# Order of weight loads, first pair and first gate weights in the feed-forward part of a one-core decoder step

## The chip, the cores and the metric

The kernel runs on one core of a Trainium2 chip as one program. TensorE (PE) multiplies matrices, VectorE (DVE), ScalarE (ACT) and GpSimd (POOL) do elementwise work, SyncE (SP) issues most DMAs and ScalarE some. Each engine works off its own list of instructions in order and waits on semaphores. The metric is the device time of one execution in microseconds, median of several runs; less is better.

## The reference

One decoder layer for 1024 prompt tokens and 8 decode tokens, 1024 channels, all float32. The part that matters here is its second half:

```python
h = h + jnp.einsum('btnd,de->bte', g * pb, w_out)          # output projection

u = rmsnorm(h, g_mlp) @ w_up                               # matrix one, 1024 x 4096
h = h + jnp.square(jax.nn.relu(u)) @ w_down                # matrix two, 4096 x 1024

h = h + (p_l @ w_ple) * jax.nn.sigmoid(rmsnorm(h, g_ple) @ w_ple_gate)
return rmsnorm(h, g_final)
```

In front of it stand the input projections, stick-breaking attention, mLSTM and a short convolution, with paged caches for the decode tokens. The change doesn't touch them.

## The kernel before

**Arithmetic.** Every float32 product is made of three faster ones: each operand is rounded to a high part (`fp32r`) and the rest is its low part, and hi x hi, hi x lo and lo x hi are summed in PSUM. So all weights and activations are rounded (ScalarE or GpSimd) and subtracted (GpSimd or VectorE) before TensorE takes them.

**Matrix one and two** (`FeedForward`, from L1970) use a recursion with seven block products in place of eight (`PRODUCTS`, L1801: 1, 5, 6, 2, 7, 3, 4), over token halves, feature halves and channel halves. The 1032 tokens are two halves of 516, each taken in two pieces of 258. A *pair* is 256 output channels. Matrix one has 16 pairs (`UPS`), n = 0 to 15, each 7 products of 24 matmuls. Matrix two has 8 groups (`DOWN_GROUPS`) of 4 pairs (q = 0 to 3), each 7 products of 12 matmuls. For the seven products of a pair VectorE forms four sums of quarters of the raw weights (`form_sum`, L2039), ScalarE rounds seven weights (`round_weight`, L2067), GpSimd makes five low parts and VectorE two (`low_part`, L2056). Four weight slots are reused within a pair, so rounding waits for an earlier product.

**Activations.** The plain operands (products 1, 2, 3) and mixed ones (5, 6, 7, 4) of the normalised input lie in SBUF as `z_plain` and `z_mixed`. The mixed ones are differences of token halves (`form_operand`, L2142) that ScalarE rounds (`t_hi`, L2382) and VectorE subtracts (`t_lo`, L2653). After each pair of matrix one, VectorE adds what belongs together and applies the ReLU and the norm (`open_11`, `open_22`, `open_12`, `open_21`), ScalarE squares, VectorE forms differences (`mixed`), and seven operands are rounded and subtracted (`u_hi`, `u_lo`) into four slots `h[:, 4:8]`. From there SyncE stores them to the DRAM tensor `feed_forward_operands` (L2134, 516 KB each). `u_hi` waits until the slot's earlier store has landed. For matrix two ScalarE's queue issues the loads of a group's seven operands (`load_operand`, L2136, 1032 KB each); half b = 0 or 1 of `z_plain` and `z_mixed` is filled while the other is used. The first group's loads follow the products of the last pair of matrix one (`first_load`); the second group's are issued in pair q = 1 of the first group (`first_extra`).

**Raw weights.** Matrix one uses two buffers of 1 MB by turns (`raw_even`, and `w_raw` as `raw_odd`), matrix two half of each (512 KB a pair). SyncE's order in the loop (L2182 to L2188) is: load of pair n+2, stores 1 to 6 of pair n, store 0 of pair n+1, load of pair n+3, and so on. Each load waits for the low parts of the buffer's former pair.

**Around it.** `MixOut` (L1839) is the output projection: eight blocks of 128 channels, three chunks of tokens. VectorE adds each chunk to the residual, ScalarE rounds the block, VectorE subtracts, ScalarE squares and scales it, VectorE sums the squares, and SyncE stores the block to `residual`. After every second block VectorE forms the mixed differences. GpSimd splits the block weights. Behind it the first pair starts: `split_first` on GpSimd (L2080), two roundings and the `t_hi` on ScalarE (L2388 to L2419), a product order as in all pairs, the norm's three sums of squares by matmul after product 1 (L2291), and three roots on ScalarE (`root`). Before the stores of pair 0 go on, SyncE loads back `h[:, 0:4]` (L2181, 2 MB). In the last group `finish` rounds and squares each finished quarter and GpSimd adds the squares; `split_landed` (L108) then splits the first gate weights, block `e0`, on GpSimd, and `gates(0)` (L2942) begins.

## Time and profile before

| | us |
|---|---|
| median of 3 runs | 2052.49 (2048.16 to 2055.67) |
| the profiled execution | 2053.93 |
| its span | 2052.2 |
| TensorE busy | 1947.3 (95%) |
| VectorE busy | 1156.5 (56%) |
| GpSimd busy | 743.7 (36%) |
| ScalarE busy | 683.7 (33%) |

The output projection ends at 1152.5 us, matrix one runs from there to 1533.4 and matrix two to 1898.5. In the profile a row of a timeline is start, duration, engine, line, operation, output<-inputs, and in brackets how long the engine was idle before it and what ended that. PE is a matmul, SPq and ACTq a DMA issue. Matmuls overlap, so their durations are longer than their distance. All lines are those of the kernel before.

### The profile page before, as it was taken

To read this page: it belongs to the slowest core of one execution; us is meant where nothing else is said; L and a number is where in the kernel's file an instruction comes from. 1 tells how busy PE (TensorE), PEld (TensorE's weight loads), DVE (VectorE), ACT (ScalarE), POOL (GpSimd) and SP (SyncE) were. 2 spreads that over 40 slices of the span, in tenths; PEclk is the share of its full clock that TensorE was granted. 3 is DMA by queue.
4 is the path that set the end of the run, shared out by engine and by line. 5 is a ranking of instruction groups with operands and counts; after the bars stand their busy time and mean duration, and the time that the engine had idled before them with its cause. 6 is when DMAs were issued, how large, how long until landed. Compare 5 with 4: busy or idle time off the path is not lost.

```text
span 2052.2 us, 37980 instructions
## 1 busy us (share of the span) xinstructions
PE 1947.3 (95%) x13592; PEld 1899.3 (93%) x13592; DVE 1156.5 (56%) x1769; ACT 683.7 (33%) x1327; POOL 743.7 (36%) x580
## 2 busy tenths in 40 slices
PE   8999999999999999999999789999985999999897
PEld 7999999999999999999999789899885999999897
DVE  5101443456454666535565667767763666678357
ACT  5112333321112222222232444454543344446212
POOL 2323222222232222234472334444442344447523
PEclk9999999999999999999999999999997999999998
DMA  3441111135533565577563156566679557661313
GB/s 116 134 134 38 51 52 63 62 95 176 154 117 114 164 184 160 163 151 226 181 207 103 52 182 220 203 217 207 205 281 347 187 197 254 243 233 43 112 32 124
DMA packets 246847, 317.42 MB, mean 155 GB/s; under 512 B 19613, under 2 KB 179465, under 8 KB 238804
## 3 DMA queue, kind: packets, MB, share of 16 engines
q1 hardware_dynamic: 223028, 234.67, 36.8%
q10 hardware_dynamic: 23712, 81.31, 11.2%
q8 instruction: 69, 1.13, 0.2%
q14 instruction: 38, 0.31, 0.0%
HBM read 219.46 MB, written 96.50 MB: 154 GB/s over the span
## 4 chain that ended last, share of the span: by engine, by line
PE 22%; issue 13%; POOL 8%; DMA 3%; DVE 3%; ACT 1%; POOLq 0%; DVEq 0%; SPq 0%; ACTq 0%
POOL w_lo L2059 6%; PE acc L142 5%; PE turned_banks L2121 5%; PE acc L2959 4%; PE acc L2121 3%; PE n_sums L2121 3%; DMA w_raw<-in_w_down 1%; POOL h L2223 1%; PE n_sums L2979 1%; DMA feed_forward_operands<-h 1%; DMA raw_even<-in_w_down 1%; DVE h L2153 1%; PE turned_banks L2998 0%; DVE h L2692 0%; POOL sq_sum L2259 0%
## 5 line engine op out<-in xcount | busy, mean ns | idle before, releaser
L142 PE MATMUL acc<-x_hi,w_hi 128*128 128x344 f32 x1680 | 546.0, 325 | 1.8 <-DVEq L1796 1.2
L142 PE MATMUL acc<-x_hi,w_lo 128*128 128x344 f32 x1680 | 537.4, 320 | 0.0
L142 PE MATMUL acc<-x_lo,w_hi 128*128 128x344 f32 x1680 | 536.9, 320 | 0.0
L112 POOL TENSOR_SCALAR w_hi<-w_raw 128x1024 fp32r<-128x1024 f32 (+1 forms) x110 | 114.3, 1039 | 671.0 <-PE acc L142 465.6
L2121 PE MATMUL turned_banks<-z_mixed,w_hi 128*128 128x258 f32 x1536 | 293.3, 290 | 46.4 <-DVE w_lo L2059 14.6
L142 PEld LDWEIGHTS acc<-x_hi,w_hi 128*128 128x128 f32 x1680 | 316.6, 188 | 3.2 <-issue 2.3
L142 PEld LDWEIGHTS acc<-x_lo,w_hi 128*128 128x128 f32 x1680 | 316.4, 188 | 0.0
L142 PEld LDWEIGHTS acc<-x_hi,w_lo 128*128 128x128 f32 x1680 | 316.2, 188 | 0.0
L2121 PEld LDWEIGHTS turned_banks<-z_mixed,w_hi 128*128 128x128 f32 x1536 | 241.3, 193 | 56.9 <-ACT kept_products L2328 15.6
L115 POOL TENSOR_TENSOR w_lo<-w_raw,w_hi 128x1024 fp32r<-128x1024 f32 (+1 forms) x110 | 248.2, 2256 | 9.2
L2121 PE MATMUL turned_banks<-z_mixed,w_lo 128*128 128x258 f32 x768 | 219.5, 286 | 0.0
L2121 PE MATMUL acc<-z_plain,w_hi 128*128 128x258 f32 x1024 | 193.8, 288 | 12.1 <-POOL w_lo L2059 11.5
L2121 PEld LDWEIGHTS acc<-z_plain,w_hi 128*128 128x128 f32 x1024 | 161.6, 193 | 15.2 <-issue 10.8
L2059 POOL TENSOR_TENSOR w_lo<-weight_sums,w_hi 128x256 fp32r<-128x256 f32 (+1 forms) x96 | 96.6, 1006 | 155.4 <-ACT w_hi L2078 155.4
L2121 PEld LDWEIGHTS turned_banks<-z_mixed,w_lo 128*128 128x128 f32 x768 | 148.1, 193 | 0.0
L2121 PE MATMUL acc<-z_plain,w_lo 128*128 128x258 f32 x512 | 146.2, 286 | 0.0
L2059 POOL TENSOR_TENSOR w_lo<-raw_even,w_hi 128x256 fp32r<-128x256 f32 (+1 forms) x72 | 79.2, 1100 | 97.9 <-ACT w_hi L2078 97.9
L2059 POOL TENSOR_TENSOR w_lo<-w_raw,w_hi 128x256 fp32r<-128x256 f32 (+1 forms) x72 | 77.5, 1076 | 98.4 <-ACT w_hi L2078 98.4
L2356 ACT ACTIVATE h<-quadrants 128x516 fp32r<-128x516 f32 (+1 forms) x96 | 67.1, 699 | 100.1 <-DMA feed_forward_operands<-h 66.8
L2121 PE MATMUL n_sums<-z_mixed,w_hi 128*128 128x258 f32 x512 | 95.3, 284 | 3.9 <-issue 2.5
L2121 PEld LDWEIGHTS acc<-z_plain,w_lo 128*128 128x128 f32 x512 | 98.8, 193 | 0.0
L2121 PE MATMUL n_sums<-z_plain,w_hi 128*128 128x258 f32 x512 | 95.2, 285 | 0.0
(365 smaller groups left out, 3720.1 us busy)
## 6 DMA issues: line engine op xcount, KB each, us to landing
feed_forward_operands<-h SPq DMA_DIRECT2D x112, 516.0 KB, 3.9
z_mixed<-feed_forward_operands ACTq DMA_DIRECT2D x32, 1032.0 KB, 6.8
w_raw<-in_w_in SPq DMA_DIRECT2D x64, 512.0 KB, 4.3
z_plain<-feed_forward_operands ACTq DMA_DIRECT2D x24, 1032.0 KB, 5.4
page<-in_cache_k SPq DMA_DIRECT2D x64, 256.0 KB, 3.2
page<-in_cache_v SPq DMA_DIRECT2D x64, 256.0 KB, 2.7
merge_gate<-merge_gates SPq DMA_DIRECT2D x22, 516.0 KB, 3.7
merge_gates<-gate_out ACTq DMA_DIRECT2D x18, 516.0 KB, 3.8
```

The costliest lines, as they stand in the source:

```text
L112: nc.gpsimd.tensor_scalar(k.w_hi[:, par, 0:kb, :], k.w_raw[:, par, 0:kb, :], 1.0, 1.0, ALU.mult, ALU.mult).then_inc(k.w_rounded, 1)
L115: nc.gpsimd.tensor_tensor(k.w_lo[:, par, 0:kb, :], k.w_raw[:, par, 0:kb, :], k.w_hi[:, par, 0:kb, :].bitcast(F32), ALU.subtract).then_inc( ...
L142: mm = k.nc.tensor.matmul(k.acc[:, c, 0:CW], w[:, par, i, :], x[:, i, cols], start=(i == 0 and j == 0), stop=(i == kb - 1 and j == 2))
L2059: op(self.slot(pair, o, self.k.w_lo), self.weight_source(pair, o), self.slot(pair, o, self.k.w_hi).bitcast(F32), ALU.subtract).then_inc(se ...
L2121: mm = nc.tensor.matmul(self.bank(j)[:, e, 0:UNIT], w[:, i, :], x, start=(fresh and i == 0 and step == 0), stop=(i == len(tiles) - 1 and s ...
L2153: self.k.nc.vector.tensor_tensor(out, at(a), at(b), ALU.subtract).then_inc(self.s["t_ready"], 1)
L2223: op(h[:, 4 + r, HALF:TT].bitcast(F32R), quads[:, quad, :], h[:, 4 + r, 0:HALF], ALU.subtract)\
L2356: nc.scalar.activation(h[:, 4 + first:4 + first + count, 0:HALF].bitcast(F32R), self.quads[:, quad:quad + count, :], ACT.Copy)\
L2959: mm = nc.tensor.matmul(k.acc[:, bank_of(u), 0:n], w[:, par, i, :], x[:, i, cols], start=(i == 0 and step == 0), stop=(i == KD - 1 and ste ...
L2979: mm = nc.tensor.matmul(emb_bank(u)[:, 0:n], w[:, i, m * P:(m + 1) * P], x[:, i, cols], start=(i == 0 and step == 0), stop=(i == KP - 1 an ...
```

## The change

Names change with it: a helper `after(n, j)` gives the number of products done when product j of pair n is, because the first pair now has an order of its own; parameters named `after` become `following`. The moves are these.

- SyncE in matrix one: the load of pair n+3 is issued after store 5 of pair n, ahead of store 6 of pair n and store 0 of pair n+1. The load of pair 2 goes ahead of the 2 MB `residual` load.
- Matrix two's raw weights: pair q has a buffer of its own (halves of `raw_even` for q = 0, 1, of `w_raw` for q = 2, 3), with its own semaphore, and each load waits for the pair four before it. The first two are loaded before the stores of pair 14 end, the next two before the stores 1 to 6 of pair 15.
- In the last pair of matrix one, ScalarE's roundings `u_hi(last, 0)` and `u_hi(last, 1)` go behind the operand loads. VectorE and GpSimd leave more of that pair's remainder to the first pairs of matrix two. The second group's seven loads spread over pairs 1 to 3.
- First pair: product order 1, 5, 2, 6, 7, 3, 4. GpSimd forms all four sums first, squares the last block and adds its squares. Two weights are rounded, and the operand of product 5 is rounded and subtracted, before the last block's own rounding. The norm's sums follow product 2.
- In the output projection the differences of blocks 2k-2, 2k-1 are formed at the start of block 2k+1, and `scale_block` stands ahead of the next block's rounding.
- The first gate weights go to `raw_even`, ScalarE rounds and VectorE subtracts them in pair q = 2 of the last group.

```diff
+                if b % 2 and b > 1:
+                    for j in (5, 7, 6, 4):
+                        ffn.form_operand(dve, j, b // 2 - 1)
...
+                    if b == KD - 1 and c == 0:
+                        ffn.form_operand(dve, 5, KD // 2 - 1)
                 dve.drain().then_inc(s["h_done"], 1)
+                if b == KD - 1:
+                    ffn.before_last_split(dve)
...
+    def square_last(self, pool, op):
+        pool.wait_ge(self.s["h_done"], KD)
+        pool.wait_ge(self.s["sq_added"], KD - 1)
+        op(self.squares, self.h[:, KD - 1, :], self.h[:, KD - 1, :], ALU.mult).then_inc(self.s["squared"], 1)
+    def add_last(self, pool, op):
+        pool.wait_ge(self.s["squared"], KD)
+        op(self.k.sq_sum[:, :], self.k.sq_sum[:, :], self.squares, ALU.add).then_inc(self.s["sq_added"], 1)
...
+            if b:
+                self.scale_block(act, b - 1)
+            if b == KD - 1:
+                ffn.before_last_rounding(act)
...
+FIRST_PRODUCTS = (1, 5, 2, 6, 7, 3, 4)
+FIRST_WEIGHTS = (0, 1, 3, 2, 4, 5, 6)
...
+def after(n, j):
+    order = FIRST_PRODUCTS if is_first(n) else PRODUCTS
+    return n * NPROD + order.index(j) + 1
...
-        if pair.par:
-            return self.k.w_raw[:, 1, :, :].rearrange("p k n -> p (k n)").rearrange("p (k n) -> p k n", n=2 * P)
...
-        return self.raw_even[:, 0:4, :]
+        if pair.q < 2:
+            return self.raw_even[:, 4 * pair.q:4 * pair.q + 4, :]
+        return self.k.w_raw[:, pair.q - 2, :, :].rearrange("p k n -> p (k n)").rearrange("p (k n) -> p k n", n=2 * P)
...
-            act.wait_ge(s["product"], pair.n * NPROD + (o - 2 if o < 3 else -1 if o == 3 else o - 3))
+            act.wait_ge(s["product"], after(pair.n - (o < 4), PRODUCTS[{0: 4, 1: 5, 2: 6, 3: 3, 4: 0, 5: 1, 6: 2}[o]]))
...
+    def before_last_rounding(self, act):
+        first = self.up(0, 0, 0)
+        self.round_weight(act, first, 0)
+        self.round_weight(act, first, 1)
+        act.wait_ge(self.k.acc_ready, self.base * NCH + 2 * NCH)
+        self.t_hi(act, 5, 0)
+        self.t_hi(act, 5, 1)
+    def before_last_split(self, dve):
+        self.t_lo(dve, 5, 0)
+        self.t_lo(dve, 5, 1)
...
-        stores(0, 0, 0, (0,))
+        load(self.up(2, 0, 1))
         sp.wait_ge(s["t_lo"], 8)
         sp.dma_start(self.h[:, 0:4, :], self.k.h_back[:, 0:4, :]).then_inc(self.h_in[0], 16)
-        with sp.Fori(0, UPS // 2 - 1) as i:
-            load(self.up(i * 2 + 2, 0, i + 1))
-            stores(i * 2, i, 0, range(1, NPROD))
-            stores(i * 2 + 1, i, 1, (0,))
-            load(self.up(i * 2 + 3, 1, i + 1))
-            stores(i * 2 + 1, i, 1, range(1, NPROD))
-            stores(i * 2 + 2, i + 1, 0, (0,))
+        stores(0, 0, 0, (0,))
+        def pair_stores(n, g, kt, loads):
+            stores(n, g, kt, range(1, 6))
+            for pair in loads:
+                load(pair)
+            stores(n, g, kt, (6,))
+            stores(n + 1, g + kt, 1 - kt, (0,))
+        with sp.Fori(0, UPS // 2 - 2) as i:
+            pair_stores(i * 2, i, 0, [self.up(i * 2 + 3, 1, i + 1)])
+            pair_stores(i * 2 + 1, i, 1, [self.up(i * 2 + 4, 0, i + 2)])
         last = UPS - 1
-        load(self.down(0, 0, 0))
-        stores(last - 1, last // 2, 0, range(1, NPROD))
-        stores(last, last // 2, 1, (0,))
-        load(self.down(0, 0, 1))
-        stores(last, last // 2, 1, range(1, NPROD - 1))
-        load(self.down(0, 0, 2))
+        half = UPS // 2 - 1
+        pair_stores(last - 3, half - 1, 0, [self.up(last, 1, half)])
+        pair_stores(last - 2, half - 1, 1, [])
+        sp.wait_ge(s["w_lo"], last * 5)
+        for q in range(2):
+            self.load_raw(sp, self.down(0, 0, q))
+        pair_stores(last - 1, half, 0, [])
+        sp.wait_ge(s["w_lo"], UPS * 5)
+        for q in range(2, OUTS):
+            self.load_raw(sp, self.down(0, 0, q))
+        stores(last, half, 1, range(1, NPROD - 1))
...
-        load(self.down(0, 0, 3))
+        def down_load(g, b, q):
+            pair = self.down(g, b, q)
+            sp.wait_ge(s["w_lo"], pair.n * 5 - 15)
+            self.load_raw(sp, pair)
...
+        for i in range(1, 5):
+            self.form_sum(pool, op, first, i)
+        low(first, 0)
+        low(first, 1)
+        self.mix.square_last(pool, op)
+        low(first, 3)
+        self.mix.add_last(pool, op)
+        for o in (2, 4, 5, 6):
+            low(first, o)
...
+        u_lo(last, 0)
+        low(down0, 5)
+        low(down0, 6)
...
+            if j == 2:
                 pe.wait_ge(self.mix.s["sq_added"], KD)
-                for (cols, _), bank in zip(self.PIECES, self.norm_sums):
-                    nc.tensor.matmul(bank, k.ones[:, :], k.sq_sum[:, cols], start=True, stop=True).then_inc(s["n1_summed"], 1)
...
+        t_hi(act, 7, 0)
         root(0)
-        keep_5(0)
+        t_hi(act, 7, 1)
         self.round_weight(act, p0, 4)
         root(1)
+        t_hi(act, 4, 0)
         root(2)
+        self.round_weight(act, p0, 5)
         keep_u2(0)
-        t_hi(7, 0)
-        t_hi(7, 1)
-        self.round_weight(act, p0, 5)
+        t_hi(act, 4, 1)
         self.round_weight(act, p0, 6)
-        t_hi(4, 0)
-        t_hi(4, 1)
...
         first_load(5)
-        u_hi(last, 1)
         square(last, 2, 1)
         self.round_weight(act, down0, 2)
         first_load(6)
-        def down_pair(pair, after, extra, first=False):
+        u_hi(last, 0)
...
+        second_load = {(1, 4): 0, (1, 6): 1, (2, 1): 2, (2, 3): 3, (2, 5): 4, (3, 1): 5, (3, 3): 6}
...
+                if (q, o) == (2, 3):
+                    act.wait_ge(k.w_landed[0], self.gate_block // 2 * 16 + 16)
+                    act.wait_ge(s["product"], (UPS + g * OUTS) * NPROD)
+                    nc.scalar.activation(k.w_hi[:, 0, :, :], self.gate_raw(), ACT.Copy).then_inc(k.w_rounded, 1)
...
+        operand(dve, 7, KD // 2 - 1)
+        operand(dve, 6, KD // 2 - 1)
+        t_lo(dve, 6, 0)
+        t_lo(dve, 6, 1)
+        operand(dve, 4, KD // 2 - 1)
+        t_lo(dve, 7, 0)
+        t_lo(dve, 7, 1)
+        t_lo(dve, 4, 0)
         form_sum(p1, 1)
-        t_lo(4, 0)
+        t_lo(dve, 4, 1)
         form_sum(p1, 2)
-        t_lo(4, 1)
...
+        left = {(0, 1): (lambda: u_lo(last, 1),), (0, 2): (lambda: mixed(last, 0), lambda: mixed(last, 1)),
+                (0, 3): (lambda: u_lo(last, 2),), (0, 4): (lambda: u_lo(last, 3),),
+                (0, 6): (lambda: u_lo(last, 4), lambda: mixed(last, 2))}
...
+                if (q, o) == (2, 6):
+                    dve.wait_ge(k.w_rounded, self.gate_block + 1)
+                    nc.vector.tensor_tensor(k.w_lo[:, 0, :, :], self.gate_raw(), k.w_hi[:, 0, :, :].bitcast(F32), ALU.subtract)\
+                      .then_inc(k.w_split, 1)
...
-            gate_weights(0)
+            sp.wait_ge(done["w_lo"], (ALL - OUTS + 1) * 5)
+            sp.dma_start(ffn.gate_raw(), w_gate[:, :, 0:P]).then_inc(k.w_landed[0], 16)
...
-            split_landed(k, pool, e0, 0, e0 // 2)
```

## Rows read from the trace of the kernel before

**Rows 1.** Table of windows: stretch, length, busy us by engine, granted PE clock, DMA.
```profile
1152.50:1190.00 37.50, 27.12 (x179) 25.21 (x178) 29.64 (x28) 23.51 (x34) 17.65 (x11) 0.86 0.04 15
1190.00:1217.90 27.90, 22.09 (x170) 21.68 (x169) 17.14 (x21) 11.81 (x21) 9.51 (x8) 0.94 0.69 240
1217.90:1239.60 21.70, 20.88 (x170) 20.28 (x168) 16.27 (x21) 11.64 (x22) 9.52 (x8) 1.00 0.64 212
1239.60:1488.40 248.80, 233.20 (x1849) 224.49 (x1849) 176.00 (x210) 123.16 (x221) 113.28 (x78) 1.00 0.62 210
1488.40:1511.90 23.50, 21.25 (x168) 20.43 (x168) 15.90 (x20) 11.07 (x21) 10.19 (x8) 1.00 0.60 200
1511.90:1533.40 21.50, 20.70 (x169) 20.35 (x169) 14.66 (x18) 8.50 (x15) 9.31 (x7) 1.00 0.91 335
1533.40:1608.50 75.10, 47.67 (x337) 46.37 (x338) 33.13 (x56) 22.54 (x50) 18.52 (x22) 0.80 0.73 276
1608.50:1648.80 40.30, 39.50 (x330) 39.30 (x329) 26.89 (x47) 16.84 (x40) 16.29 (x20) 1.00 0.65 232
```
**Rows 2.** Waits, 1239.6 to 1488.4: total us, times, longest us.
```profile
ACT h L2356 <- DMA feed_forward_operands<-h: 36.4, 11, 4.0
DVE acc L2054 <- DMA raw_even<-in_w_up: 33.3, 6, 5.8
DVE acc L2054 <- DMA w_raw<-in_w_up: 28.0, 5, 6.1
```
**Rows 3.** DMA issues, 1239.6 to 1488.4: size and median us to landing.
```profile
feed_forward_operands<-h SPq DMA_DIRECT2D x77, 516.0 KB, 3.8
raw_even<-in_w_up SPq DMA_DIRECT2D x6, 1024.0 KB, 7.0
w_raw<-in_w_up SPq DMA_DIRECT2D x5, 1024.0 KB, 7.4
```
**Rows 4.** Timeline of one steady pair of matrix one, which starts at 1397.45.
```profile
1400.02 0.39 SPq L2065 DMA_DIRECT2D w_raw<-in_w_up  x1
...
1407.60 0.70 DVE L2054 TENSOR_TENSOR acc<-w_raw 128x512 f32<-128x512 f32 x1 [5.47 <-DMA w_raw<-in_w_up]
...
1408.97 0.64 ACT L2356 ACTIVATE h<-quadrants 128x516 fp32r<-128x516 f32 x1 [3.34 <-DMA feed_forward_operands<-h]
...
1416.84 0.69 DVE L2587 TENSOR_TENSOR quadrants<-n_sums,kept_products 128x516 f32<-128x516 f32 x1
...
1420.02 0.50 PE L2121 MATMUL acc<-z_plain,w_hi 128*128 128x258 f32 x2 [0.65 <-POOL w_lo L2059]
...
1426.27 0.52 PE L2121 MATMUL turned_banks<-z_mixed,w_hi 128*128 128x258 f32 x2 [0.23 <-ACT turned_banks L2319]
```
**Rows 5.** Timeline around the last two projection blocks and the first pair.
```profile
1130.66 2.41 POOL L115 TENSOR_TENSOR w_lo<-w_raw,w_hi 128x1024 fp32r<-128x1024 f32 x1
1131.07 3.10 DVE L1915 SCALAR_TENSOR_TENSOR z_plain<-h,g_mlp_c,z_plain 128x1032 fp32r<-128x1032 f32 x1 [1.28 <-ACT z_plain L1939]
...
1154.52 1.29 DVE L1915 SCALAR_TENSOR_TENSOR z_plain<-h,g_mlp_c,z_plain 128x1032 fp32r<-128x1032 f32 x1 [1.27 <-ACT z_plain L1939]
...
1157.43 1.05 ACT L2386 ACTIVATE z_mixed<-h 128x1032 fp32r<-128x1032 f32 x1
...
1158.80 0.77 PE L2280 MATMUL turned_banks<-z_plain,w_hi 128*128 128x258 f32 x2 [6.11 <-POOL w_lo L2059]
```
**Rows 6.** DMA view, 1510 to 1610, in 40 slices, and one timeline row.
```profile
GB/s 149 74 247 295 422 429 405 391 373 409 419 410 423 391 414 251 9 245 384 295 316 390 262 412 426 423 423 419 414 407 402 259 28 0 0 0 0 0 145 71
DMA packets 9559, 28.08 MB, mean 281 GB/s; under 512 B 592, under 2 KB 3664, under 8 KB 7504
...
1591.09 0.43 DVE L2054 TENSOR_TENSOR acc<-w_raw 128x256 f32<-128x256 f32 x1 [15.72 <-DMA w_raw<-in_w_down]
```
**Rows 7.** Timeline between matrix two and the first gate.
```profile
1902.16 0.75 DVE L2778 SCALAR_TENSOR_TENSOR z_lo<-h,g_ple_c,z_mixed 128x516 fp32r<-128x516 f32 x1 [0.80 <-ACT z_mixed L2538]
...
1905.13 2.34 POOL L115 TENSOR_TENSOR w_lo<-w_raw,w_hi 128x1024 fp32r<-128x1024 f32 x1
...
1907.53 0.69 PE L2959 MATMUL acc<-z_mixed,w_hi 128*128 128x384 f32 x1 [8.99 <-POOL w_lo L115]
```

More of the change, by code:

```diff
@@ L2043, in form_sum @@
         if i == 1:
-            eng.wait_ge(self.raw_in[pair.par], pair.half * 16 + 16)
+            eng.wait_ge(*self.landed(pair))
         if i in (2, 4):
@@ L2224, in u_lo, with steady @@
                 .then_inc(s["u_lo_pool"], 1)
-        def steady(pair, after):
+        def steady(pair, following):
             for o in (2, 3, 5, 6):
@@ L2229, in steady @@
             u_lo(pair.n - 1, 6)
-            low(after, 0)
+            low(following, 0)
             u_lo(pair.n, 0)
-        self.split_first(pool, self.up(0, 0, 0))
+        first = self.up(0, 0, 0)
+        for i in range(1, 5):
[7 more added lines that the diff above has]
+            low(first, o)
         low(self.up(1, 1, 0), 0)
@@ L2239, in gpsimd @@
         last = UPS - 1
-        steady(self.up(last, 1, UPS // 2 - 1), self.down(0, 0, 0))
         for o in (2, 3, 5, 6):
-            low(self.down(0, 0, 0), o)
+            low(self.up(last, 1, UPS // 2 - 1), o)
+        u_lo(last - 1, 6)
+        down0 = self.down(0, 0, 0)
+        for o in (0, 2, 3):
+            low(down0, o)
+        u_lo(last, 0)
+        low(down0, 5)
+        low(down0, 6)
         u_lo(last, 6)
@@ L2357, in u_hi, with steady @@
               .then_inc(s["u_hi"], 1)
-        def steady(pair, after):
+        def steady(pair, following):
             n = pair.n
@@ L2581, in open_whole, with open_sum @@
               .then_inc(s["read"], 1)
-        def open_sum(n, o, j, kept, other, quad, i):
-            dve.wait_ge(s["product"], n * NPROD + o)
+        def open_sum(n, j, kept, other, quad, i):
+            dve.wait_ge(s["product"], after(n, j))
             dve.wait_ge(s["kept"], n * 3 + kept)
@@ L2631, in u_lo, with steady @@
                                     h[:, 4 + first:4 + first + count, 0:HALF], ALU.subtract).then_inc(s["u_lo"], 1)
-        def steady(pair, after):
+        def steady(pair, following, spare=None):
             n = pair.n
@@ L2706, in next_sum @@
             def next_sum(i):
-                if after is not None:
-                    form_sum(after, i)
+                if following is not None:
+                    form_sum(following, i)
             previous()
@@ L2728, in down_pair @@
             add_read(n, 6, 3, 2 * q, 1)
-            if after is not None:
-                low_part(after, 1)
+            if following is not None:
+                low_part(following, 1)
             extra(6)
@@ L2755, in group @@
                     previous = before_q
[L2756 removed]
+                down_pair(pair, following, previous, extra(q))
         for q in range(OUTS):
```

210 lines of the change are left out of this document (104 added, 106 removed).

## The prediction, made before the changed kernel was run

> **What bounds the kernel now.** I read the page's slices first: TensorE is busy nearly throughout, so only its holes and stretches of lower granted clock can be won. The table of windows, cut at the borders of the stages, then says where the holes are. The group stage of matrix two, undisturbed, runs four pairs (336 matmuls) in 40.3 us [rows 1]: 0.12 us a matmul, so 20.2 us for a pair of matrix one (168 matmuls) and 10.1 us for a pair of matrix two (84). Against this, eleven steady pairs of matrix one take 248.8 us, 22.6 each [rows 1], though no engine but TensorE is full (VectorE 176.0 us, GpSimd 113.3). The first pair takes 37.5 us counted from the last projection matmul, the second 27.9, the last one and the first four of matrix two 96.6 (21.5 + 75.1) instead of 20.2 + 40.3 = 60.5 [rows 1].
>
> The list of waits for the steady stretch shows what is late: VectorE waits 33.3 + 28.0 us for raw weights, 5.6 us in each of eleven pairs, and ScalarE 36.4 us for stores [rows 2]. A load lands after 7.0 to 7.4 us, a store after 3.8 [rows 3]. In the timeline the load of the pair after next is issued at 1400.02, lands at 1407.60 and holds VectorE 5.47 us. The store issued just behind it holds ScalarE until 1408.97. From then VectorE works without a hole, opens the last sum at 1416.84, and weights for the next pair come late on GpSimd; TensorE starts the next pair at 1420.02 [rows 4].
>
> **Part 1, steady pairs.** Before, the load of pair m stands in SyncE's queue behind the store of operand 0 of pair m-2. Now it stands behind operand 5 of pair m-3 and waits only for the low parts of pair m-2. Nothing is added or dropped: each pair has its 1 MB load and seven stores. I laid out the queues of one pair at 20.2 us, from its first matmul as zero. The last raw weights of a pair are split at about 11.5 us, so the load is issued there and has until 4 us into the next pair, 12.7 us; it needs 7.4 [rows 3]. VectorE's 5.6 us wait goes. The two stores that now stand behind the load (operands 6 and 0) become ready at 15 and 18 us, later than the load's issue, and are needed at 3.4 and 5.9 us of the next pair: 8 us each against 3.8 [rows 3]. The store of operand 1 no longer shares the engines with a load.
>
> What is late next? The longest chain is the one around the pair's end: open the last sum, finish the quadrants, differences, round, then seed the bank of product 6. It runs from 1416.84 to 1426.27, 9.43 us [rows 4], of which about 0.8 us is waiting for ScalarE and GpSimd, which are early once VectorE is. That leaves 8.6 us, and three products give TensorE 8.65. So it just fits; VectorE has 16.0 us of work in 20.2. I take 20.4 us a pair, between 20.2 (no hole) and 21.5 (the chain stays at 9.4 and another hole of 0.5 remains). The pair before the eleven and the eleven are 21.7 + 248.8 = 270.5 us [rows 1], and 12 x 20.4 = 244.8: **25.7 us**, bounds 12 and 28. The last pair but one, 23.5 [rows 1] to 20.3: **3.2 us**.
>
> **Part 2, first pair.** The stall of 6.11 us before the first matmul is for a weight that ScalarE rounds only after block 7 [rows 5]. Now two weights, the first two rounded halves of the operand of product 5 and both their low parts lie inside the last projection block, where ScalarE waits for chunks. What is left is the last chunk's add, 0.9 us. The low parts of the operand of product 5 are VectorE's and start when GpSimd squares the last block. A GpSimd instruction over 1024 columns took 2.41 us, and a VectorE one of the same width started 0.4 us later took 3.10 us instead of 1.29 [rows 5]: it ended 1.1 us after GpSimd. So the low part waits for the square, and product 5 starts 2 us after product 1 ends. The Trainium skill states this as a rule (SBUF — State Buffer, "Who interferes with whom"): two engines share a port pair, held for a whole instruction, against an instruction with two SBUF inputs. The trace agrees, 3.10 against 1.29; by the free duration the pair would be 2 us shorter.
>
> Then the order 1, 5, 2 lets the plain product run while the mixed operands are made, the norm sums come after it (about 1.3 us), and product 7 waits for the second kept product, which stands in ScalarE's queue behind three roots and four operand roundings: about 3 us. Sum from the last projection matmul: 0.9 + 20.2 + 2 + 1.3 + 3 + 2 (slower clock after the holes, half of what 0.86 granted cost before) = 29.4 instead of 37.5: **8 us**, bounds 4 and 11.
>
> The second pair had 27.9 us because the load of the third was issued behind the 2 MB residual. That load now goes first: 21 us, **7 us**, bounds 4 and 7.7.
>
> **Part 3, matrix one to matrix two.** Four raw pairs instead of two can be in flight, the first operand loads are taken ahead of two roundings in ScalarE's queue, and the second group's seven loads (7.2 MB) move from pair 1 to pairs 1 to 3. Worst before was the wait of 15.72 us for the fourth raw weights, issued into a queue full of those loads [rows 6]; that goes. What stays is the amount: 28.08 MB move between 1510 and 1610, and the transfers run at about 410 GB/s when they are dense [rows 6]. That is 68.5 us, more than TensorE's 60.5. VectorE also has the leftovers of the last pair in the first pair of matrix two (about 12 us of work in 10), so a hole of 2 to 3 us there lies beside the same time. I take the transfers as the bound: 68.5 instead of 96.6, **28 us**. Bounds: 36 at no stall, 18 if the transfers have as many thin slices as before, when they ended at about 1590 [rows 6] and group 1 could not have started sooner. The last of the second group's loads is issued some 5.5 us before group 1 starts and all seven are awaited at once, so the hole will be there.
>
> The Trainium skill (DMA: Bandwidth & Descriptors, "Queues, rings and completion order") says that SyncE's and ScalarE's queues have a ring each on the same 16 engines, which alternate between them. Then a deeper queue of raw weights brings no bytes faster, only earlier. The throughput row is flat at 373 to 429 GB/s in its dense stretches, whichever queue feeds it [rows 6]; by queues independent of each other this part would be worth 36 us.
>
> **Part 4, gate weights.** TensorE waits 8.99 us at the first gate for a GpSimd instruction that ends at 1907.47 and stands behind all its adds of squares [rows 7]. The rounding (ScalarE, 1.05 us by the row of the same size) and the subtraction (VectorE, at most 1.29 us) [rows 5], now lie in the last group's third pair. VectorE is 67 per cent busy in the undisturbed group, 26.9 us in 40.3 [rows 1], more in the last; they may cost up to 1 us there. Next late is the low part of the last quadrant, 1902.91 [rows 7], which the first gate awaits before its last block: 0.6 us. The second weights follow 3 us earlier on GpSimd, the embedding's stay where they were and are due just then. **8 us**, bounds 3 and 9.
>
> Sum: 25.7 + 3.2 + 8 + 7 + 28 + 8 = 79.9 us. The profiled execution took 2053.9 us (span 2052.2), 1.4 over the median of 2052.5; so 1974 profiled, and I forecast **1974 us**, leaving the 1.4 us to parts that I rounded up.
>
> **The rivals.** (a) The transfers are not dense at the border: stores wait for VectorE's leftovers and the second group waits for its last load. Part 3 gives 18: 1984 us. For it: between its dense stretches the throughput fell to 9 and 245 GB/s [rows 6]; against: raw weights and first loads no longer queue behind stores. (b) The steady chain does not shrink: ScalarE and VectorE run 9.4 us from the last sum to the seed and TensorE waits 0.8 us there and again for GpSimd's weight. Pairs of 21.5, 12 and 1 of them: 1988 us. Both together: 1998. (c) Slower: the load blocks SyncE. It waits for all low parts of the pair before, and the stores behind it hold ScalarE's rounding ahead of the kept product, which TensorE needs. It decides from the point where these stores land over 8 us late; to lose, each of 14 pairs must grow by 5.7 us over my 20.4, for example to 27: 2066. Against: the load's condition is met at 11.5 us, those stores are ready at 15. (d) The load doesn't move: the low parts it waits for end together with the store that it stood behind, so part 1 goes: 2003. Against: GpSimd is through with them and does three more instructions before that store is ready.
>
> **Numbers.** Forecast 0.50, (a) 0.18, (b) 0.15, both 0.06, (d) 0.05, (c) 0.02, better than forecast 0.04 (all bounds good: 1958). The range 1958 to 2001 leaves out less than 2 in 10. One measurement of this kernel tells about 0.3% (6 us) from no change: faster 0.96, same 0.02, slower 0.02.
>
> **What would show it.** Steady pairs of 20.2 to 20.6 us and no wait of VectorE for raw weights; the first matmul of matrix one within 1 us of the last projection matmul; a hole before product 7 of the first pair; one hole, of a few us, before group 1 of matrix two, with transfers near 410 GB/s until then; the first gate within 1 us of the last product. Wrong would be: pairs above 21.5, ScalarE still waiting for stores, or several holes of over 3 us behind 1533.

## The result, and the profile after

The changed kernel takes 1980.1 us (median of 4 runs, 1976.5 to 1981.1), the kernel before 2053.4 us in the same comparison: a ratio of 0.9643, 95% interval 0.9621 to 0.9666. Forecast was 1974 us in a range of 1958 to 2001. The profiled execution has a span of 1979.3 us, 72.9 less than before.

The table of windows of the changed kernel, cut at the same borders as [rows 1] (stretch, length, busy us of TensorE, its weight loads, VectorE, ScalarE and GpSimd with their counts, granted clock, DMA share, GB/s):

```profile
1152.90:1183.80 30.90, 25.06 (x180) 23.36 (x180) 25.89 (x24) 21.27 (x32) 16.87 (x9) 0.94 0.25 92
1183.80:1203.90 20.10, 20.10 (x169) 20.10 (x169) 16.81 (x20) 11.82 (x20) 10.62 (x7) 1.00 0.81 287
...
1225.90:1466.10 240.20, 240.20 (x2004) 240.20 (x2003) 203.59 (x227) 141.08 (x239) 130.62 (x84) 1.00 0.66 231
1466.10:1486.30 20.20, 20.20 (x171) 20.20 (x170) 14.17 (x19) 10.29 (x19) 8.87 (x6) 1.00 1.02 376
1486.30:1511.20 24.90, 13.95 (x84) 13.38 (x82) 14.04 (x21) 9.26 (x19) 6.45 (x8) 0.79 0.89 346
1511.20:1546.30 35.10, 32.29 (x254) 32.09 (x255) 21.69 (x36) 12.65 (x30) 14.24 (x17) 0.95 0.93 346
1546.30:1586.60 40.30, 40.30 (x326) 40.30 (x326) 26.22 (x45) 15.78 (x38) 15.70 (x18) 0.96 0.66 231
```

What to see: from 1183.8 to 1486.3 TensorE is busy as long as the stretch is, in every row. The steady pairs have no hole left. The stretch that took 75.1 us before [rows 1] is the fifth and sixth row here, 24.9 + 35.1 = 60.0 us, with TensorE busy in only 46.2 of them and a granted clock of 0.79 in the first. This is what is left of the stalls, most of it in and just behind the first pair of matrix two.

By the starts of TensorE's products, the gain is made up of: projection to second pair 37.6 to 30.9 us (6.7); second pair 27.9 to 20.2 (7.8); the 14 pairs behind it 315.5 to 282.4 (33.1, of which 1.3 in the last pair); the first four pairs of matrix two 75.1 to 60.0 (15.1); the rest of matrix two 0.6; the tail from the start of the last product of matrix two to the end 155.3 to 145.6 (9.7). The projection ended 0.25 us later, which leaves 72.8; the spans rounded give 72.9.

The list of waits of the steady stretch of the changed kernel, 1225.9 to 1466.1 (total us, times, longest us), its three longest:

```profile
POOL w_lo L2113 <- ACT w_hi L2132: 73.9, 48, 2.4
ACT quadrants L2442 <- DVE quadrants L2674: 40.4, 18, 3.3
POOL h L2306 <- ACT h L2456: 36.4, 12, 3.0
```

The three rows of [rows 2], waits for raw weights and for stores, are not in it, though loads and stores take as long as before; the view of the DMA issues of the same stretch:

```profile
feed_forward_operands<-h SPq DMA_DIRECT2D x83, 516.0 KB, 3.8
w_raw<-in_w_up SPq DMA_DIRECT2D x6, 1024.0 KB, 6.8
raw_even<-in_w_up SPq DMA_DIRECT2D x5, 1024.0 KB, 6.9
```

Against [rows 3] the times from issue to landing are nearly the same (3.8, 6.8 and 6.9 us against 3.8, 7.4 and 7.0); what changed is when the loads are issued.

In the first pair of matrix two the timeline of the changed kernel shows where TensorE stands:

```profile
1488.97 0.63 ACT L2456 ACTIVATE h<-quadrants 128x516 fp32r<-128x516 f32 x1 [2.26 <-DMA feed_forward_operands<-h]
...
1491.06 0.49 PE L2162 MATMUL turned_banks<-z_mixed,w_hi 128*128 128x258 f32 x2 [1.99 <-ACT turned_banks L2419]
...
1494.89 0.63 ACT L2456 ACTIVATE h<-quadrants 128x516 fp32r<-128x516 f32 x1 [3.67 <-DMA feed_forward_operands<-h]
...
1500.75 0.77 PE L2162 MATMUL turned_banks<-z_mixed,w_hi 128*128 128x258 f32 x2 [5.05 <-ACT kept_products L2428]
...
1509.16 1.32 POOL L2306 TENSOR_TENSOR h<-quadrants,h 128x516 fp32r<-128x516 f32 x1 [7.23 <-ACT h L2456]
...
1511.21 0.51 PE L2162 MATMUL acc<-z_plain,w_hi 128*128 128x258 f32 x2 [3.93 <-POOL w_lo L2113]
```

ScalarE's roundings at 1488.97 and 1494.89 write the slots that pair 14's stores are read from, and wait for those stores: the one issued at 1477.44 took 17.4 us and landed at 1494.81, just ahead of the second rounding. The seed and the copies that TensorE needs stand behind these roundings in ScalarE's queue, so the first two stalls go back to stores. The third, ahead of the second pair, does not do so directly: GpSimd's low part of the weights stands behind the last pair's operand (the row at 1509.16), which waited 7.23 us for ScalarE's rounding, and that rounding for VectorE's difference. This is the leftover work of the last pair.

A *hole* is, in what follows, the distance from the start of the last matmul before it to the first one behind it, less the 0.12 us that two matmuls are apart at full speed. It is some 0.15 us longer than the idle time in brackets, which counts from a modelled end (0.47 longer behind the norm's matmuls).

The view of the transfers from 1466.3 to 1546.3 (40 slices of 2 us) shows the rest:

```profile
GB/s 244 236 370 430 426 404 414 419 405 416 423 418 414 425 417 381 379 349 58 383 386 281 74 256 316 155 281 413 400 390 407 408 420 401 406 409 407 425 378 133
DMA packets 10204, 28.31 MB, mean 354 GB/s; under 512 B 607, under 2 KB 4693, under 8 KB 8150
```

Behind the first three slices the transfers are dense, at about 412 GB/s, until 1502, thin until 1520, and dense again until the group's operands have landed. At 412 the 28.31 MB are 68.7 us; they took 80.

### The profile page after: what moved, and what is told of

Read it like the earlier page. It is cut to its first block and busy times, and to the rows that moved or that the text cites. A ratio compares the mean times of both kernels' runs of the same rounds, so it can differ in the third digit from the quotient of the medians.

```text
span 1979.3 us, 37940 instructions
## 1 busy us (share of the span) xinstructions
PE 1926.6 (97%) x13592; PEld 1890.7 (96%) x13592; DVE 1181.8 (60%) x1769; ACT 693.0 (35%) x1327; POOL 760.1 (38%) x580
## 3 DMA queue, kind: packets, MB, share of 16 engines
q1 hardware_dynamic: 223028, 234.67, 37.6%
q10 hardware_dynamic: 23712, 81.31, 11.7%
## 5 line engine op out<-in xcount | busy, mean ns | idle before, releaser
L2162 PE MATMUL turned_banks<-z_mixed,w_hi 128*128 128x258 f32 x1536 | 286.4, 285 | 15.2 <-ACT kept_products L2428 8.0
L2113 POOL TENSOR_TENSOR w_lo<-weight_sums,w_hi 128x256 fp32r<-128x256 f32 (+1 forms) x96 | 111.8, 1164 | 186.0 <-ACT w_hi L2132 186.0
L2113 POOL TENSOR_TENSOR w_lo<-w_raw,w_hi 128x256 fp32r<-128x256 f32 (+1 forms) x72 | 81.7, 1135 | 48.1 <-ACT w_hi L2132 48.1
L142 PE MATMUL acc<-y_hi,w_hi 128*128 128x344 f32 x288 | 93.3, 324 | 1.9 <-POOL w_lo L115 1.1
```

The costliest lines, as they stand in the source:

```text
L142: mm = k.nc.tensor.matmul(k.acc[:, c, 0:CW], w[:, par, i, :], x[:, i, cols], start=(i == 0 and j == 0), stop=(i == kb - 1 and j == 2))
L2113: op(self.slot(pair, o, self.k.w_lo), self.weight_source(pair, o), self.slot(pair, o, self.k.w_hi).bitcast(F32), ALU.subtract).then_inc(se ...
L2162: mm = nc.tensor.matmul(self.bank(j)[:, e, 0:UNIT], w[:, i, :], x, start=(fresh and i == 0 and step == 0), stop=(i == len(tiles) - 1 and s ...
```

## The experiments

All ran against the kernel before; ratios are to it, the changed kernel having 0.9643. "Four pairs" is the time from the first product of matrix two to the first one of its group 1, from the profile. The intervals are 3 to 5 us wide to each side, so where kernels differ by less the profile decides.

**Undo the order of SyncE's queue (e5).**

```diff
-            stores(n, g, kt, range(1, 6))
-            for pair in loads:
-                load(pair)
-            stores(n, g, kt, (6,))
+            stores(n, g, kt, range(1, 7))
             stores(n + 1, g + kt, 1 - kt, (0,))
+            for pair in loads:
+                load(pair)
```

> Only SyncE's order in matrix one's loop is put back: the load of the raw weights stands behind the last store of its pair and the first store of the next, instead of ahead of them. Nothing is left out. If the order of SyncE's queue is what the steady pairs gained by, the pairs go back from 20.17 us to 22.0 to 22.6, on 11 to 13 pairs, and the time is 2004 to 2012. If the pairs gained by something else (product order, the shorter chain around the first pair, fewer waits), they stay at 20.2 to 20.6 and the time is 1979 to 1985.

2011.1 us, ratio 0.9798 (0.9775 to 0.9820): 31.8 us of the gain gone. Twelve pairs that took 242.0 us take 268.2, 22.35 each. The waits of 1230 to 1470 in this kernel are those of [rows 2] again, within a microsecond:

```profile
ACT h L2455 <- DMA feed_forward_operands<-h: 37.1, 11, 3.7
DVE acc L2108 <- DMA raw_even<-in_w_up: 33.3, 6, 5.9
DVE acc L2108 <- DMA w_raw<-in_w_up: 27.7, 5, 5.8
```

So the place of the load, ahead of two stores or behind them, is the cause of the steady gain. Matrix one, first pair included, lost 36.5 us, but the four pairs at the border took 55.3 instead of 60.0 us. I take it that slower pairs ahead leave less in flight at the border; no run tests that.

**Undo the hand-over of the gate weights (e6).**

```diff
# ScalarE's and VectorE's parts in the last group taken out; GpSimd, behind its last add of squares (waits left out here):
+        nc.gpsimd.tensor_scalar(k.w_hi[:, 0, :, :], self.gate_raw(), 1.0, 1.0, ALU.mult, ALU.mult).then_inc(k.w_rounded, 1)
+        op(k.w_lo[:, 0, :, :], self.gate_raw(), k.w_hi[:, 0, :, :].bitcast(F32), ALU.subtract).then_inc(k.w_split, 1)
```

> The first gate weights (128x1024) are rounded and split by GpSimd behind its last part of matrix two, as in the kernel before, instead of by ScalarE and VectorE inside the last group; the load keeps its new place and buffer. Nothing is left out. If the 9.7 us that the tail gained come from this hand-over, they go back: the first gate product starts 8 to 11 us later than 1.5 us after the last product of matrix two; time 1987 to 1992. If they come from the earlier load alone: 0 to 3 us; time 1979 to 1983.

1989.2 us, ratio 0.9687 (0.9666 to 0.9708): 9.0 us. The timeline of this kernel has a row like that of [rows 7] again:

```profile
1841.74 2.34 POOL L2373 TENSOR_TENSOR w_lo<-raw_even,w_hi 128x1024 fp32r<-128x1024 f32 x1
...
1844.14 0.69 PE L3053 MATMUL acc<-z_mixed,w_hi 128*128 128x384 f32 x1 [9.30 <-POOL w_lo L2373]
```

The early load alone gives nothing; the engine that splits does.

**ScalarE's copies first (e1).** The roundings of the last pair's operands move behind the copies in all three engines' queues.

```diff
-        left = {(0, 0): square(last, 3, 2), (0, 1): u_hi(last, 1), (0, 2): u_hi(last, 2), (0, 3): u_hi(last, 3), ...
+        left = {(0, 0): square(last, 3, 2), (0, 3): u_hi(last, 0), (0, 5): u_hi(last, 1), (1, 0): u_hi(last, 2), ...
```

> ScalarE's roundings of the last pair's operands (u_hi of the pair before matrix two) stand behind the seed and the two copies of the first pair of matrix two, instead of ahead of them; VectorE's and GpSimd's parts of the same chain move with them. Nothing is left out. Theory 1 (order): the holes of the first pair (2.15, 5.20 and 4.09 us) come from ScalarE, which waits in order for stores to land while TensorE waits for the copies behind. Then the first pair takes 10 to 13 us instead of 24.9, what waits next is the residual, and the four pairs of group 0 take 52 to 56 us instead of 60.0; time 1972 to 1976. Theory 2 (bytes): the transfers are the bound whatever the order; the holes move to the second and third pair, where VectorE waits for the residual, and the four pairs stay within 58.5 to 61.5; time 1978 to 1982.

1978.4 us, 0.9631 (0.9615 to 0.9647), four pairs 59.4 us. Both totals lie in the ranges of theory 2. Of the mechanism each theory got half: the first pair falls from 25.2 to 14.8 us as theory 1 said, and the third rises from 10.1 to 19.7, as theory 2 said. In this kernel's timeline VectorE then stands for the residual, and TensorE behind it:

```profile
1513.31 0.34 SPq L2275 DMA_DIRECT2D h<-residual  x1
...
1522.70 0.70 DVE L2788 TENSOR_TENSOR h<-turned_banks,h 128x516 f32<-128x516 f32 x1 [9.95 <-DMA h<-residual]
...
1524.22 0.77 PE L2162 MATMUL turned_banks<-z_mixed,w_hi 128*128 128x258 f32 x2 [7.72 <-ACT turned_banks L2420]
```

**The second group's loads early (e2), and both (e3).**

```diff
-        second_load = {(1, 4): 0, (1, 6): 1, (2, 1): 2, (2, 3): 3, (2, 5): 4, (3, 1): 5, (3, 3): 6}
+        second_load = {(1, o): o for o in range(NPROD)}
```

> The seven loads of the second group's operands are issued in the second pair of matrix two, one at each product, as in the kernel before, instead of being spread from the second pair to the fourth. Nothing is left out. Theory 3 (spread): the transfers are thin from 1501 to 1520 us and the hole of 2.96 us ahead of group 1 is the price of the spreading; then the hole goes, the thin stretch fills, and the four pairs take 55 to 57.5 us instead of 60.0; time 1975 to 1977. Theory 2 (bytes) and theory 1: the seven loads (1 MB each) run beside the last stores and the residual, which land later, and VectorE waits for the residual at the third pair: 61 to 66 us; time 1981 to 1986.

> The edits of the two runs before together: ScalarE's copies first, and the second group's loads in the second pair. Nothing is left out. Theory 1: 48 to 54 us for the four pairs, since the second pair now starts some 12 us earlier and the second group's loads with it; time 1968 to 1974. Theory 2 (bytes): what the one gains the other takes: 58 to 62 us; time 1978 to 1983.

e2: 1978.1 us, 0.9637 (0.9621 to 0.9653), four pairs 58.9 us. The hole ahead of group 1 is gone, a smaller one came in the fourth pair. It gained 1 us of the 2.5 to 5 that theory 3 asked, and had none of the loss that the other two forecast; all three missed. e3: 1986.4 us, 0.9676 (0.9660 to 0.9693), four pairs 67.7 us, worse than any theory said. With ScalarE early the seven loads meet the last stores. The view of the DMA issues of e3, 1494 to 1544 (count, KB each, median us to landing), and then the timeline of its longest wait:

```profile
z_mixed<-feed_forward_operands ACTq DMA_DIRECT2D x4, 1032.0 KB, 9.1
feed_forward_operands<-h SPq DMA_DIRECT2D x6, 516.0 KB, 11.0
```

```profile
1530.69 0.69 DVE L2788 TENSOR_TENSOR h<-turned_banks,h 128x516 f32<-128x516 f32 x1 [17.73 <-DMA h<-residual]
...
1532.21 0.77 PE L2162 MATMUL turned_banks<-z_mixed,w_hi 128*128 128x258 f32 x2 [13.48 <-ACT turned_banks L2420]
```

A store of 0.5 MB takes 11.0 us there against 3.8 in the steady pairs; the residual load has to wait for it in SyncE's queue, and VectorE for the residual.

**Fewer bytes (e4).**

```diff
-        act.dma_start(self.ops.rows(j, b, 0, 0, 4).bitcast(F32), src).then_inc(sem, 16)
+        act.dma_start(self.ops.rows(j, b, 0, 0, 4)[:, 0:rows, :].bitcast(F32), src[:, 0:rows, :]).then_inc(sem, 16)   # rows=1 for group 0
```

> Each of the seven loads of the first group's operands carries one of its four rows (0.26 instead of 1.06 MB); the other three rows of group 0's operands are left as they were, so this part of matrix two is not computed from its data. 5.5 MB less at about 400 GB/s is 14 us of transfer. Theories 1 and 2 (contention): pair 14's stores land in 4 us, as in the steady pairs, instead of 8, ScalarE doesn't wait, and the four pairs take 43 to 48 us instead of 60.0; time 1962 to 1968. Theory 4 (the stores are late by themselves, by the order in which SyncE issues them, six in 17 us): ScalarE waits as before, the holes of the first pair stay above 8 us, and the four pairs take 55 us or more.

1973.9 us, 0.9617 (0.9600 to 0.9633), four pairs 55.0 us. That is outside the range of theories 1 and 2 and at the edge of theory 4's, but of ScalarE's waits for stores in the first pair (2.26 and 3.67 us) only one of 1.27 us is left, against theory 4. 5.4 MB less gave 5 us, not 14. Stores issued from 1461 to 1495 landed in 4.8 us (median) instead of 10.0 in the changed kernel (1466 to 1500), so it is shown that the stores are late because of the loads beside them. But TensorE still had holes of 3.08 us ahead of product 7 and 3.83 ahead of the second pair, now behind the last pair's differences and roundings themselves. In this kernel's timeline:

```profile
1489.05 1.06 ACT L2456 ACTIVATE h<-quadrants 128x1032 fp32r<-128x1032 f32 x1 [2.87 <-DVE quadrants L2720]
...
1490.74 0.77 PE L2162 MATMUL turned_banks<-z_mixed,w_hi 128*128 128x258 f32 x2 [2.93 <-ACT kept_products L2428]
```

**The wait for the residual later (e7), and that with fewer bytes (e8).**

```diff
-            if q != 1:
-                dve.wait_ge(self.h_in[q == 2], 48 if q == 3 else 32)
             down_pair(...)
# and inside down_pair, after next_sum(2):
+            before_add()      # the same wait, ahead of add_kept
```

> The edit of e1 (ScalarE's copies first) with one more: VectorE's wait for the residual stands directly ahead of the first addition that needs it, instead of ahead of the whole pair (there it also held the last addition of the pair before, whose end ScalarE's seed waits for, and the sums of weights). Nothing is left out. Theory 2, as a chain: in e1 the second residual load was issued at 1513.3 us and landed at 1522.7, and TensorE stood 7.9 us. With the wait later TensorE goes two to three products further; 3 to 5 of the 7.9 us go, the four pairs take 54 to 57 us instead of 59.4, time 1973 to 1976. If the residual isn't what bounds (rather the sum of bytes up to group 1), the time comes back ahead of group 1: 58 to 60 us, time 1977 to 1980.

> The kernel of e7 with the small loads of e4 (each of the seven loads of group 0's operands carries one of its four rows; that group's product isn't computed from its data). If order and bytes together explain the 20 us that the four pairs take above their 40.3 at full speed, both are gone here: 41 to 46 us for the four pairs; time 1959 to 1965. If a third thing holds them (GpSimd's low parts, the clock), 50 us or more as in e4 (55.0).

e7: 1979.0 us, 0.9637 (0.9617 to 0.9658), four pairs 61.7 us. The third pair fell to 13.8 us, from e1's 19.7, the fourth rose to 21.6, from 12.3: the time came back ahead of group 1, as the second case said, and a little more than it said. e8: 1976.4 us, 0.9622 (0.9600 to 0.9644), four pairs 61.0 us: 15 us above the first range, so the second case in number (50 or more), and slower there than e4, from which it differs only in the two edits of order. In e8 the first pair took 10.4 us, full speed; then the second group's loads, issued from 1506.35 by a ScalarE that was now early, ran beside the last store (issued 1509.62; the residual load that waits for it went out at 1525.88), and the next raw weights stood in SyncE's queue behind both:

```profile
1525.88 0.34 SPq L2275 DMA_DIRECT2D h<-residual  x1
...
1526.67 1.22 SPq L2119 DMA_DIRECT2D raw_even<-in_w_down  x2
...
1537.13 0.43 DVE L2108 TENSOR_TENSOR acc<-raw_even 128x256 f32<-128x256 f32 x1 [11.65 <-DMA raw_even<-in_w_down]
```

**The second group's loads behind the residual (e9), and raw weights ahead of it (e12).**

```diff
# e9, over e7
+        second_load = {(2, 3): 0, (2, 4): 1, (2, 5): 2, (2, 6): 3, (3, 0): 4, (3, 1): 5, (3, 2): 6}
# e12, over e7
+        second_load = {(1, 1): 0, (1, 3): 1, (2, 3): 2, (2, 4): 3, (2, 5): 4, (2, 6): 5, (3, 0): 6}
+        down_load(1, 1, 0)
         residual(0, self.h_in[1])
         stores(last, last // 2, 1, (NPROD - 1,))
+        down_load(1, 1, 1)
         residual(2, self.h_in[0])
```

> The kernel of e7 with the second group's seven operand loads issued later: the first at the fourth product of the third pair of matrix two, the last early in the fourth, one at each step. Nothing is left out. Theory 5 (SyncE's chain): in e7 and e8 the last stores and the residual took 9 to 16 us to land beside these loads (1 MB each), and behind the wait for them stood the second residual load (issued 1528.7) and the next raw weights (landed 1540.2). With the loads behind the residual, the stores land in 4 to 5 us again, the third pair doesn't stand, and what is left is the landing of the second group: seven loads of 2.6 us from about 1518, so 1537 to 1541 on e7's clock: the four pairs take 50 to 55 us instead of 60.0, time 1970 to 1975. Theory 2 (the sum of bytes up to group 1 is the bound, whatever the order): 58 to 62 us, time 1978 to 1982.

> The kernel of e7 with two things more: SyncE issues the raw weights of group 1's first two pairs ahead of the residual loads instead of behind them (in e9 they were issued at 1516.1 beside seven operand loads and landed at 1536.5, and TensorE stood 12.3 us for them), and of the second group's seven operand loads two are issued at the start of the second pair, where the transfers were thin (240 GB/s from 1504 to 1513 in e9), and five from the middle of the third. Nothing is left out. In all four orders run so far the 80 us that end with group 1's first product carried 28.1 to 28.3 MB at 354 to 358 GB/s, where the dense slices show about 412: if thin stretches are what is left to win, this order takes up to 5 us of them: the four pairs take 53 to 57 us instead of 60.0, time 1973 to 1977. If each load that fills the thin stretch makes the last stores later by as much, as in e2 and e3, the four pairs take 59 to 62 us, and the time is 1978 to 1982.

e9: 1979.5 us, 0.9647 (0.9629 to 0.9664), four pairs 59.6 us. The stores did land early (the last issued 1508.73; the residual load behind it went out at 1515.33) and the first three pairs took 13.7, 12.0 and 10.1 us, but the raw weights behind the residual took 20.4 us to land beside the seven loads, and the fourth pair took 23.8. Theory 5 missed; both totals lie in theory 2's ranges. e12: 1981.9 us, 0.9655 (0.9641 to 0.9669), four pairs 63.2 us: the time is in its second case, the four pairs 1 us above it. The two loads at 1500.59 and 1503.38 hold the stores up, as in e3, and the second residual load is late:

```profile
1509.00 0.64 ACT L2458 ACTIVATE h<-quadrants 128x516 fp32r<-128x516 f32 x1 [4.80 <-DMA feed_forward_operands<-h]
...
1540.02 0.70 DVE L2783 TENSOR_TENSOR h<-h,kept_products 128x516 f32<-128x516 f32 x1 [8.65 <-DMA h<-residual]
```

**GpSimd beside VectorE in the first pair (e10).**

```diff
-        op(self.squares, self.h[:, KD - 1, :], self.h[:, KD - 1, :], ALU.mult).then_inc(self.s["squared"], 1)
+        pool.sem_inc(self.s["squared"], 1)
# and the addition of the square likewise
```

> GpSimd's square of the last block of the output projection and its addition to the sum of squares are left out (that block is missing from the normalisation); all the rest of the changed kernel stands. If VectorE's operations are long because GpSimd works beside them: the two t_lo of 1.84 us each fall to 1.2 to 1.4, product 5 of the first pair starts without its 0.94 us, the two differences of 2.29 us each fall to 0.7 to 1.5, and product 6 starts 1 to 1.9 us earlier; the first pair takes 28.5 to 30 us instead of 30.9. If they wait for something else (ScalarE's rounding, the scaling of the block), the durations stay and the two holes too.

One run, 1973.7 us. The timeline of the changed kernel, VectorE's rows and the GpSimd rows beside them:

```profile
1153.62 1.91 POOL L1937 TENSOR_TENSOR quadrants<-h 128x1032 f32<-128x1032 f32 x1 [3.35 <-DVEq L1918]
...
1154.08 3.68 DVE L2205 TENSOR_TENSOR z_mixed<-h,z_mixed 128x1032 fp32r<-128x1032 f32 x2 [0.58 <-ACT z_mixed L2199]
...
1160.09 2.41 POOL L1941 TENSOR_TENSOR sq_sum<-sq_sum,quadrants 128x1032 f32<-128x1032 f32 x1
...
1160.19 4.58 DVE L2194 TENSOR_TENSOR h<-h 128x516 f32<-128x516 f32 x2 [1.23 <-ACT h L1949]
```

and VectorE's two rows in e10's timeline:

```profile
1151.12 2.38 DVE L2205 TENSOR_TENSOR z_mixed<-h,z_mixed 128x1032 fp32r<-128x1032 f32 x2 [0.58 <-ACT z_mixed L2199]
...
1156.85 2.40 DVE L2194 TENSOR_TENSOR h<-h 128x516 f32<-128x516 f32 x2 [2.14 <-ACT h L1949]
```

3.68 becomes 2.38 us and 4.58 becomes 2.40, of the same two instructions each. The hole ahead of product 5 (0.94 us) is gone, that ahead of product 6 falls from 1.88 to 0.37, and the first pair, from the warm-up matmul, takes 27.3 instead of 29.85 us, both at a granted clock of 0.94 (from the last projection matmul, as the expectation counts, 28.3 instead of 30.9: a little below its range). So GpSimd's square and addition cost 2.5 us here, in two places. VectorE holds up GpSimd too: GpSimd's low part at 1158.27 took 1.85 us with VectorE's row of 1157.68 beside it (until 1158.96), and 1.31 in e10, where it ran alone. These rows agree with the Trainium skill's rule of the port pair (SBUF — State Buffer, "Who interferes with whom").

**The copy of U2 earlier (e11).**

```diff
-        root(2)
-        self.round_weight(act, p0, 5)
         keep_u2(0)
+        self.round_weight(act, p0, 5)
+        root(2)
```

> In the first pair, ScalarE's copy of U2 (keep_u2) stands ahead of the rounding of weight 5 and the last third of the root, instead of behind both. Nothing is left out. The hole of 3.2 us ahead of product 7 was waited for at this copy (idle 2.95 us, released by ScalarE). If ScalarE's order is the cause, product 7 starts 1.5 to 2.3 us earlier, and the first pair takes 28.8 to 30 us instead of 30.9, unless the root, now 1.2 us later, holds the fourth product of the bank behind it. If the operand or the low part of product 7 is as late as the copy, it stays at 30.5 or more. The time differs by less than its interval either way; the profile decides.

1979.1 us, 0.9645 (0.9628 to 0.9662). TensorE's idle time ahead of product 7 fell from 2.95 to 1.18 us and the first pair, from the warm-up matmul, from 29.85 to 27.2 us (28.2 as the expectation counts, below its range). Of the 2.6 us, 1.5 are the clock, as the last section shows. And the root, now later, gave holes of 0.56 us ahead of product 4 and 1.09 in the second pair, which rose from 20.2 to 21.4. First and second pair together take 48.6 us, as they do in e1, e2 and e3 with the old order and the same clock. No gain.

## Why the prediction was right, and where it was not

**Steady pairs**: predicted 25.7 + 3.2 us by 20.4 us a pair, measured 20.17 with no hole, 31.8 for the same pairs. The mechanism is the predicted one, shown by e5. The chain around the pair's end does fit into three products; the 0.2 us of caution, 13 times, are the difference; the twelve pairs alone gave 28.5, just above the upper bound of 28. Rivals (b), (c) and (d) did not occur.

**First pair**: predicted 8, measured 6.7; 30.9 us instead of 29.4. Its steps: product 5 came 0.94 us late, not 2, since GpSimd's square began 0.5 us ahead of VectorE and was over at 1155.5, so that it held only the first of two instructions; TensorE stood 2.95 us ahead of product 7 for the copy, as predicted (3). The step that was missing is product 6, with a hole of 1.88 us: I had counted the contention once, but the addition of the square and a low part lie beside the two differences as well (e10; what the low part alone costs was not tested). That the new order of products and weights gave the 6.7 us is read from the trace; no run puts it back.

**Second pair**: predicted 7, measured 7.8, full speed. Before, VectorE stood 9.68 us for the load issued at 1192.17, behind the 2 MB residual; now the load is issued at 1176.54, ahead of it, lands at 1181.9, and the wait is gone. No run undoes this move alone. **Gate weights**: predicted 8 with 9 as upper bound, measured 9.7; the first gate product follows the last product of matrix two without a wait, and TensorE is idle for 0.77 and 0.35 us later; e6 gives 9.0 for it.

**Border of the matrices**: the term that was mis-sized. "I take the transfers as the bound: 68.5 instead of 96.6" gave 28 us; measured were 20.2 + 60.0 = 80.2, so 16.4, which is below its own lower bound of 18. By the prediction's own signs this part was wrong: ScalarE still waited for stores there (2.26 and 3.67 us), and two holes were above 3 us. It is rival (a) with its reason: the amount was right (28.31 MB in the 80 us up to group 1), the density was not, 354 GB/s on average against 412 in the dense slices. I had put all of the hole ahead of group 1, which is 2.96 us; the others, 2.15, 5.20 and 4.09, lie in and behind the first pair of matrix two. What did come true is that VectorE's wait of 15.72 us for the fourth raw weights [rows 6], behind which TensorE had a hole of 11.7 us, is gone; which of the moves at the border did that was not tested. e2 puts one of them back, the spreading of the second group's loads, and loses nothing.

That the total came out 6 us from the forecast is in part luck: the border fell short by 11.6 us and the first pair by 1.3, and the steady pairs, the second pair, the gate weights and the rest of matrix two gave 6.0 more than forecast.

What the runs put in place of "the transfers are the bound": neither the amount nor one engine's order is. Taking 5.4 MB away gave 5 us (e4), and with two edits of order beside it nothing (e8, 61.0 us); an order of the same bytes took 67.7 (e3). Taking ScalarE's wait away gave 10 us in the first pair and lost 10 in the third (e1). What the traces show in each of these kernels is a chain through SyncE's queue: last pair's stores, which wait for the slots of the pair before; residual loads, which wait for those stores; raw weights behind both. Its links landed in 3 to 8 us with few loads beside them, and in 8 to 25 beside the 1 MB operand loads, which have a queue of their own. That this chain is the bound is my reading and not shown: no kernel removed it, and four forecasts built on it (e7, e8, e9, e12) missed, since each edit moved the wait to another link. Loads placed in the thin stretch make the links late (e3, e8, e12); loads placed behind it come late themselves (e9). Six orders of all the work gave 58.9, 59.4, 59.6, 61.7, 63.2 and 67.7 us against 60.0. The rule of the Trainium skill that the prediction weighed (DMA: Bandwidth & Descriptors, "Queues, rings and completion order") fits these rows: it says that the queues share the engines, and in e3 a store among the large loads takes 11.0 us instead of 3.8.

None of the complete kernels beat the changed one by more than its interval. Left open is whether smaller pieces (the residual in four loads, the group's products waiting for one operand each) would shorten the chain; that was not tried. Also open is how much of the thin stretch belongs to the leftover work of ScalarE, VectorE and GpSimd alone; that it holds TensorE is seen in the hole ahead of the second pair, 4.09 us and still 3.83 with the stores on time (e4).

## What to carry to other kernels

A load that waits behind a store in the same queue costs what the store waits for, not what it transfers; moving it ahead of two stores was worth 32 us here, the largest part of the 73. Where a stage is bound by bytes, look for the stretch in which the transfers are thin and ask which chain of dependent transfers crosses it: the bytes divided by the dense rate are a floor, and such a chain can keep you above it: here 80 us instead of 69. And price an engine's slow neighbour for every pair of instructions that lie side by side, not for the first.

## What the runs showed of the hardware that was not expected

The granted clock makes the same instructions take one of two times. The first pair, from the warm-up matmul on, took 28.3 us in e1, e2, e3, e4 and e8, and 29.8 to 30.9 in the changed kernel, e5, e6, e7, e9 and e12, though none of these edits touches it. The windows of e2 and of the changed kernel:

```profile
1150.60:1178.90 28.30, 23.16 (x179) 21.47 (x178) 24.61 (x22) 19.79 (x31) 16.63 (x9) 1.00 0.21 76
```

```profile
1153.90:1183.80 29.90, 24.76 (x179) 23.07 (x179) 25.37 (x23) 20.34 (x32) 16.59 (x9) 0.94 0.26 95
```

The holes are the same; in the changed kernel the granted clock fell to the lower level (1.2 GHz) after the hole ahead of product 7, which then took 4.5 us, and in e2 it stayed at full speed and product 7 took 3.0. So a difference of 1.5 us in this pair says nothing about an edit. In the changed kernel's first pair of matrix two the lower level follows the holes too: the 24.9 us hold 13.95 of matmuls at a mean clock of 0.79 which at full speed are 10.1, so the holes cost some 3.9 us more than they are long.
